# Attention scores over all 128 rows of TensorE, with the stacked operands loaded in four parts: one change in two mixing layers

## What is computed

```python
# neighbourhood: q, k of 64 features; scale 64 ** -0.5, a bias, a softmax over the near positions
s = einsum('bqhd,brqchd->bhqrc', q_row, k_nb) * scale + bias
# differential: two score maps a head, each over 32 features
s = einsum('bqhcd,bkhcd->bchqk', q_blk, k) * 32 ** -0.5 + bias
a = softmax(s)[:, 0] - lam * softmax(s)[:, 1]
# latent: 64 features and 32 rotated ones, 96 together
s = (einsum('bqhd,bkhd->bhqk', qn, k_nope) + einsum('bqhd,bkd->bhqk', qr, k_rope)) * 96 ** -0.5
```

## Time and profile before

| | |
|---|---|
| median of three runs | 1137.87 us |
| profiled execution | 1138.59 us |
| its span, first to last instruction | 1136.80 us |
| granted TensorE clock, mean | 0.999 of full |
| PE (TensorE matmul) busy | 1121.8 us, 99% |
| PEld (weight load) busy | 974.8 us, 86% |
| DVE (VectorE) busy | 782.1 us, 69% |
| ACT (ScalarE) busy | 533.3 us, 47% |
| POOL (GpSimd) busy | 60.5 us, 5% |
| DVE L971, the low part of a weight unit | 171 times, mean 2294 ns |
| DMA | 207.02 MB, mean 182 GB/s |

### The profile page before, as it was taken

The page is one execution under the profiler, slowest core; times in us unless marked ns, Lnnn a source line. Parts: engine busy times, 40 slices in busy tenths (PEclk is TensorE's granted clock), DMA queues, the critical chain, the costliest instruction groups (busy, mean ns, idle before and its releaser), DMA issues. The chain is left out here.

```text
span 1136.8 us, 16893 instructions
## 1 busy us (share of the span) xinstructions
PE 1121.8 (99%) x6556; PEld 974.8 (86%) x6556; DVE 782.1 (69%) x1015; ACT 533.3 (47%) x702; POOL 60.5 (5%) x99
## 2 busy tenths in 40 slices
PE   8999999999999999999999999999999999999997
PEld 7888888898888888879988888888899988888886
DVE  6766666767667666677676676666766866766665
ACT  5533333456653334344585533343446755333332
POOL 1000000000000000003400000000034000000000
PEclk9999999999999999999999999999999999999999
DMA  8766566664356565668733465656676244665550
GB/s 254 254 209 196 178 202 202 221 207 142 118 167 222 185 188 182 209 156 249 205 122 114 165 222 186 187 184 209 176 238 157 85 149 133 215 208 185 184 184 37
DMA packets 170295, 207.02 MB, mean 182 GB/s; under 512 B 20707, under 2 KB 153187, under 8 KB 170242
## 3 DMA queue, kind: packets, MB, share of 16 engines
q1 hardware_dynamic: 166226, 202.89, 55.8%
q0 software_dynamic: 4016, 3.42, 1.6%
HBM read 201.98 MB, written 1.16 MB: 179 GB/s over the span
## 5 line engine op out<-in xcount | busy, mean ns | idle before, releaser
L657 ACT ACTIVATE whi<-raw 128x2048 fp32r<-128x2048 f32 x176 | 336.4, 1915 | 382.6 <-PE bank L1572 245.5
L971 DVE TENSOR_TENSOR wlo<-raw,whi 128x2048 fp32r<-128x2048 f32 x171 | 391.9, 2294 | 158.3 <-ACT whi L657 158.2
L1568 PE MATMUL bank<-h_both,whi 128*128 128x512 f32 x1280 | 304.6, 390 | 0.0
L1568 PEld LDWEIGHTS bank<-h_both,whi 128*128 128x128 f32 x1280 | 237.7, 188 | 47.7
L1542 PE MATMUL bank<-whi,o_hi 128*128 128x512 f32 x448 | 176.2, 393 | 0.0
L1543 PE MATMUL bank<-wlo,o_hi 128*128 128x512 f32 x448 | 174.9, 390 | 0.0
L1544 PE MATMUL bank<-whi,o_lo 128*128 128x512 f32 x448 | 174.4, 389 | 0.0
L1572 PEld LDWEIGHTS bank<-h_both,wlo 128*128 128x128 f32 x1280 | 164.1, 191 | 6.2
L1572 PE MATMUL bank<-h_both,wlo 128*128 128x256 f32 x1280 | 166.0, 283 | 0.0
L1544 PEld LDWEIGHTS bank<-whi,o_lo 128*128 128x128 f32 x448 | 84.1, 188 | 17.9
L1542 PEld LDWEIGHTS bank<-whi,o_hi 128*128 128x128 f32 x448 | 84.3, 188 | 17.6 <-issue 1.3
(11 more groups left out here) (200 smaller groups left out, 1280.7 us busy)
## 6 DMA issues: line engine op xcount, KB each, us to landing
raw<-in_w_gate_up SPq DMA_DIRECT2D x44, 1024.0 KB, 5.1
raw<-in_w_down SPq DMA_DIRECT2D x44, 1024.0 KB, 4.9
raw<-in_w_gate SPq DMA_DIRECT2D x22, 1024.0 KB, 5.4
raw<-in_w_up SPq DMA_DIRECT2D x22, 1024.0 KB, 5.4
raw<-in_w_in SPq DMA_DIRECT2D x20, 1024.0 KB, 6.3
raw<-in_w_o SPq DMA_DIRECT2D x12, 1024.0 KB, 5.1
raw<-in_w_kv SPq DMA_DIRECT2D x8, 1024.0 KB, 5.3
raw<-in_w_q SPq DMA_DIRECT2D x4, 1024.0 KB, 5.0
```

The source lines that it names most:

```text
L657: act.activation(whi[:, s, :], raw[:, s, :], ACT.Copy).then_inc(hi_ready, 1)
L971: dve.tensor_tensor(wlo[:, s, :], raw[:, s, :], whi[:, s, :].bitcast(F32), ALU.subtract).then_inc(lo_ready, 1)
L1568: pe.matmul(bank[bk + jj][:, :], hi[:, kc, jj * P:(jj + 1) * P], h_both[:, kc, :, :].rearrange("p a t -> p (a t)"), start=(kc == 0), stop= ...
```

## The change

- **Latent**: the scores read all 128 rows of `qall`; rows 96 to 127 are set to zero once by GpSimd (`rows_zero`).
- **Neighbourhood**: ScalarE's copies of units 2 and 3 are written as fp32r, VectorE makes their low parts (`near_low`) into free tiles of `pr`, and GpSimd's DMAs stack them (`load_near`, 12 a layer): queries high over low against keys high over high (slots 6 to 9) and against keys low over low (slots 2 to 5). An item is four fp32r matmuls over 128 rows (`near_scores`) in place of two f32 ones over 64.
- **Differential**: the stacks have a fourth quarter, low against low, so 128 rows. Each DMA now moves 32 rows of one item: 64 a layer in place of 24. Since neighbourhood keys hold slots 2 to 5, 8 and 9 of `o_lo`, the keys come in four parts with a semaphore each; parts 1 and 2 are issued behind waits for scores, and TensorE waits for the part that an item needs.

```diff
-    s += unit(0) + unit(1) + unit(2) + [("mla_T",)] + unit(3) + [("mla_B",), ("mla_G",)] + unit(4)
+    s += unit(0) + unit(1) + unit(2) + [("near_low", 2), ("mla_T",)] + unit(3) + [("near_low", 3), ("mla_B",), ("mla_G",)] + unit(4)
...
+        near_hi = {2: kg[:, 1, :, :], 3: qg[:, 1, :, :]}
+        near_lo = [{2: pr[:, 7, :, :], 3: pr[:, 6, :, :]}, {2: pr[:, 3, :, :], 3: pr[:, 2, :, :]}]
+        NEAR_SLOT = 6
+        NEAR_LOW_SLOT = 2
...
-            def load_diff(l, n):
-
-                pool.wait_ge(diff_low, 2 * l + n - 3)
-                to, order = (o_lo, (diff_hi, diff_hi, diff_lo)) if n == 5 else (o_hi, (diff_hi, diff_lo, diff_hi))
-                for b, part in enumerate(order):
-                    for r in range(4):
-                        first, second = DIFF_SLOT[r], DIFF_SLOT[r + 4]
-                        pool.dma_start(to[32 * b:32 * b + 32, first:second + 1:second - first, :],
-                                       part[n][32 * r:32 * r + 32]).then_inc(diff_in, 16)
+            def load_near(l, n):
+
+                pool.wait_ge(near_low, 2 * l + n - 1)
+                hi, lo = near_hi[n], near_lo[l][n]
+                stacks = [(o_lo, NEAR_SLOT, (hi, hi)), (o_lo, NEAR_LOW_SLOT, (lo, lo))] if n == 2 else [(o_hi, NEAR_SLOT, (hi, lo))]
+                for to, slot, parts in stacks:
+                    for b, part in enumerate(parts):
+                        for r in range(2):
+                            pool.dma_start(to[HD * b:HD * b + HD, slot + r:slot + r + 3:2, :],
+                                           part[HD * r:HD * r + HD].bitcast(F32R)).then_inc(near_in, 16)
+
+            def load_diff(n, items, done):
+
+                to, order = (o_lo, (diff_hi, diff_hi, diff_lo, diff_lo)) if n == 5 else (o_hi, (diff_hi, diff_lo, diff_hi, diff_lo))
+                for i in items:
+                    c_, r = (i - 8) // 4, (i - 8) % 4
+                    for b, part in enumerate(order):
+                        pool.dma_start(to[32 * b:32 * b + 32, DIFF_SLOT[i - 8], :],
+                                       part[n][32 * r:32 * r + 32, c_, :]).then_inc(done, 16)
...
+                load_near(l, 2)
                 mask_na(l)
-                load_diff(l, 4)
-                load_diff(l, 5)
+                load_near(l, 3)
+                pool.wait_ge(diff_low, 2 * l + 1)
+                load_diff(4, range(8, 14), diff_in[0])
+                pool.wait_ge(diff_low, 2 * l + 2)
+                load_diff(5, (8, 9), diff_in[0])
+                pool.wait_ge(scores, 16 + 20 * l + 6)
+                load_diff(5, (10, 11), diff_in[1])
+                pool.wait_ge(scores, 16 + 20 * l + 8)
+                load_diff(5, (12, 13), diff_in[2])
+                load_diff(4, (14, 15), diff_in[3])
+                load_diff(5, (14, 15), diff_in[3])
...
+            pool.wait_ge(scores, 16)
+            pool.wait_ge(rstd_ready, tile_no(3, 1) + 1)
+            pool.memset(qall[MLA_D:P, :, :], 0.0).then_inc(rows_zero, 1)
+            pool.wait_ge(rows_zero, 1)
...
+                    elif k == "near_low":
+
+                        n = ev[1]
+                        dve.wait_ge(proj_out, p0 + n - 1)
+                        dve.scalar_tensor_tensor(out=near_lo[l][n].bitcast(F32R).rearrange("p a b -> p (a b)"), in0=bank[mix_bank(n)][:, :],
+                                                 scalar=1.0 if n == 2 else HD ** -0.5,
+                                                 in1=near_hi[n].rearrange("p a b -> p (a b)"),
+                                                 op0=ALU.mult, op1=ALU.subtract).then_inc(near_low, 1)
...
+            def near_scores(i, h, bank_free):
+
+                pe.wait_ge(bank_free, i - 1)
+                for qt in range(2):
+                    dst, q = bank[i % 2][:, qt * T:(qt + 1) * T], o_hi[:, NEAR_SLOT + h, qt * P:(qt + 1) * P]
+                    pe.matmul(dst, q, o_lo[:, NEAR_SLOT + h, :], start=True, stop=False)
+                    mm = pe.matmul(dst, q, o_lo[:, NEAR_LOW_SLOT + h, :], start=False, stop=True)
                 mm.then_inc(scores, 1)
...
-                        pe.wait_ge(proj_out, p0 + 1)
+                        pe.wait_ge(near_low, 2 * l + 1)
...
+                            pe.wait_ge(rows_zero, 1)
...
-                            q, kk = qall[0:MLA_D, i, :], qall[0:MLA_D, 4 + i, :]
+                            q, kk = qall[:, i, :], qall[:, 4 + i, :]
...
-                                pe.wait_ge(diff_in, 16 * 24 * (l + 1))
-                                q, kk = o_hi[0:96, DIFF_SLOT[i - 8], :], o_lo[0:96, DIFF_SLOT[i - 8], :]
+                                part = (i - 8) // 2
+                                pe.wait_ge(diff_in[part], 16 * (32, 8, 8, 16)[part] * (l + 1))
+                                q, kk = o_hi[:, DIFF_SLOT[i - 8], :], o_lo[:, DIFF_SLOT[i - 8], :]
...
-                        scores_of(i0 + i, q, kk, False, exped if 2 <= i < 6 else maxed)
+                        if 4 <= i < 8:
+                            pe.wait_ge(near_in, 16 * 12 * (l + 1))
+                            near_scores(i0 + i, i - 4, exped if i < 6 else maxed)
+                        else:
+                            scores_of(i0 + i, q, kk, False, exped if 2 <= i < 6 else maxed)
```

More of the change, by code:

```diff
@@ L287, in bass_two_stacks @@
         na_ready = sem("na_ready")
-        diff_low, diff_in = sem("diff_low"), sem("diff_in")
+        rows_zero = sem("rows_zero")
+        diff_low, diff_in = sem("diff_low"), [sem("diff_in%d" % k) for k in range(4)]
+        near_low, near_in = sem("near_low"), sem("near_in")
         consts_set, pad_set, vec_done, vec_out = sem("consts_set"), sem("pad_set"), sem("vec_done"), sem("vec_out")
@@ L897, in mix @@
                                 dst = diff_hi[n].bitcast(F32R).rearrange("p a b -> p (a b)")
+                            if n in near_hi:
+                                dst = near_hi[n].bitcast(F32R).rearrange("p a b -> p (a b)")
                             scale = 1.0
@@ L1837, in scores_of @@
                 mm.then_inc(scores, 1)
+            def near_scores(i, h, bank_free):
[4 more added lines that the diff above has]
+                    mm = pe.matmul(dst, q, o_lo[:, NEAR_LOW_SLOT + h, :], start=False, stop=True)
+                mm.then_inc(scores, 1)
             def transpose_head(q, i, causal):
```

## The result

The changed kernel took **1141.13 us** (median of 14 runs, 1140.36 to 1142.63), the kernel before in the same comparison 1138.23 (14 runs, 1137.45 to 1140.39): a ratio of 1.0024, with a 95% interval of 1.0018 to 1.0031. The change makes the kernel 2.9 us slower. I had forecast 0.5 us less.

What follows compares the result with a forecast made beforehand. TensorE's matmuls, busy 99% of the span, were taken as the bound. Neighbourhood scores gain 0.5 us, latent and differential nothing, all else hidden: 1137.4 us from the median 1137.87, range 1136.6 to 1139.2.

Steps and rivals of the forecast that it cites:

- the sum: Whole kernel: profiled 1138.59 us less 0.5 is 1138.1; the same 0.5 off the three-run median 1137.87 gives 1137.4 us.
- GpSimd's queue, the part with a risk: Mixing layers: one memset, 12 neighbourhood and 64 differential DMAs a layer, all hidden; both ends kept, 0 to 2.6 us.
- Neighbourhood scores: TensorE, mixing layers: fp32r pairs save 0.12 and 0.13 us, together 0.25 us a layer, 0.5 us for two.
- Latent and differential scores over 128 rows: TensorE, mixing layers: 128 rows cost what 96 do, so 0 gained or lost in either kind of score.
- GpSimd's queue inside the layer: Second mixing layer: 3.9 us or more spare before the differential series, 2.0 us spare at part 3, no wait.
- The short wait: Rival: the gain is absent, or part 3 lands up to 1 us late; 1137.9 to 1139.5 us, chance 0.13.
- the late series: Rival: differential issues take 0.55 us or more, part 3 misses, 3.9 us of wait a layer; 1145 us, chance 0.07.
- the locked-out issues: Rival: VectorE's multiplies each stop GpSimd's series for their length, 4.1 to 7.4 us a layer; 1145.6 to 1152.2, chance 0.03.
- The rule that I weighed: Differential series: VectorE operations in 2-port mode lock GpSimd out of writing descriptors; taken as a small effect at most.
- VectorE, ScalarE, volume of the transfers: Mixing layers: two added 0.68 us VectorE operations a layer, 1.5 us spare; 4 MB more DMA for both layers, free.

## Why the prediction was wrong

**The step that failed** is the sum's silence on what GpSimd's transfers cost at the end of the program. Under "GpSimd's queue, the part with a risk" I priced each transfer by its issue and its landing and asked only who waits for it in the mixing layer. The same 104 transfers have a third price, paid in the closing DRAIN: 0.0817 us for each that is still counted, 40 more of these than before, 3.26 us. The rows were to be had. The chain that ended last passed `POOLq L184`, and the list of that line has the DRAIN ending 0.65 us after SyncE was ready, so every tenth of a microsecond added to GpSimd's end was a tenth in the time; I read the middle of the kernel, found TensorE busy for 99%, and took it that the last microseconds belonged to TensorE too. "A microsecond saved on another engine is worth nothing" was false for the one engine that closes the program. No rival had it either: all of mine that ended slower were waits in the mixing layer.

Could it have been priced? Not from the trace of before alone, which has one DRAIN with one number of transfers. A bound from both sides could have been had: between nothing and 4.93 / 52 = 0.095 us each, 0 to 9.9 us for 104. That would have moved both the range and the chance of slower.

**Neighbourhood scores**: right. 0.12 us in each pair, 0.24 to 0.25 a layer in the starts of matmuls with the same number, 0.5 in all (forecast 0.25 and 0.5).

**Latent and differential scores over 128 rows**: right, nothing. 1.89 us against 1.89, 0.58 against 0.57.

**GpSimd's queue inside the layer**: right, with room to spare. These rows are its timeline in the second layer:

```profile
842.37 2.40 POOL L623 DMA_DIRECT2D o_lo<-kg  x4
...
847.04 5.54 POOL L613 TENSOR_TENSOR bias<-bias,nmask 128x256 f32<-128x256 f32 x8
...
862.73 0.57 POOL L632 DMA_DIRECT2D o_hi<-qg  x1 [7.87 <-DVE xn L1540]
863.29 0.51 POOL L632 DMA_DIRECT2D o_hi<-xn  x1
...
893.27 1.04 POOL L632 DMA_DIRECT2D o_lo<-xn  x2
```

A neighbourhood issue takes 0.60 us (2.40 / 4; taken: 0.52 to 0.73). GpSimd waits 7.9 us before the differential series, which needs (893.81 - 862.73) / 63 = 0.493 us an issue, not 0.52; the last ends at 894.3, where I had it end at some 897.1. TensorE comes to item 14 at 899.85 and does not wait. The short wait, the late series and the locked-out issues all did not come.

**The rule that I weighed.** Of the 128 issues of the two series nine took over 0.52 us, the longest 0.60, beside a median of 0.50. Each of the nine lies under one of VectorE's multiplies and ends 0.10 us after it. One of them, and the two multiplies over it:

```profile
871.02 0.59 POOL L632 DMA_DIRECT2D o_hi<-xn  x1
...
870.89 0.62 DVE L1299 TENSOR_SCALAR pr<-pr,rsum 128x256 f32<-128x256 f32 x2
```

Such an issue lost a tenth of a microsecond, and most issues beside a multiply lost nothing: the next one, 871.60 to 872.10, has multiplies beside it from 871.62 on. At most 0.35 us go with the pause before the 133rd transfer, if that is their doing. The Trainium skill, page "SBUF — State Buffer", section "SBUF: two separate sides", says that GpSimd cannot write descriptors while a VectorE operation in a 2-port mode runs. The trace agrees with that in part, in where the nine issues end; whether the multiplies run in such a mode no run here shows. What I had made of it, that each multiply adds its whole length to the series, did not come.

**Reading the DRAIN.** It is 8.19 us long where it starts over 50 us after the last transfer was issued, with one power of 0.56 us beside it on its engine, so its length is not a wait for a transfer to land. The Trainium skill, page "Perfetto Trace Analysis", section "Sequencer-only Instruction (DRAIN, etc)", says that the recorded start of such an instruction is when its semaphores are satisfied. The trace agrees: here the DRAIN starts with the last power (947.49 and 947.53), once what GpSimd had waited for was there, and its record holds none of the wait before it.

**VectorE, ScalarE, volume of the transfers**: nothing appeared, as forecast; TensorE's list of waits has no new entry.

## What to carry to other kernels

Before pricing a change, follow the chain that ended last to its very end, and read the rows of the program's last line as well: behind the last matmul each engine closes its own queue, and the one that closes last is a bound that the share of busy time doesn't show. Here each DMA that GpSimd issued anywhere in the program, up to 128 of them, cost 0.08 us there, whatever its size, so that 104 more small copies, 40 of them still counted, for a gain of 0.5 us were a loss; give GpSimd no work at the end of a kernel that issues many DMAs from it, and its closing runs beside other work (1137.07 us, the fastest of all kernels here). And a theory that fits three sizes of one kind (more rows, more transfers) still has to be tried with the two taken apart.

## What the runs showed of the hardware that I had not expected

- GpSimd's closing DRAIN takes 0.68 us, of which 0.59 are the last power and the 0.04 us before it, and 0.0817 us for each transfer on its queue, equal for 1 row of 256 bytes and for 128 rows of 8, to 0.01 us over six counts from 52 to 128.
- It never came to more than 11.13 us: 128 transfers seem to be what is kept. Past that, issuing more can make it shorter: 156 gave 4.60 us in one kernel, 8.19 in another.
- Issues from GpSimd: 0.48 to 0.50 us for 32 rows of 1 KB, 0.60 for 128 rows, 0.48 for one row. Nine of the 128 in the series were held up, by up to 0.10 us, and each of the nine ends 0.10 us after a multiply of VectorE.
- Scores over 96 and over 128 rows take the same time, 1.89 us for 8 instructions.
